# Meta keys of the attention turned by transposes, a Silu and a split moved ahead of the gates' casts, input squares on ScalarE

## The reference

```
h = rms_norm(x); z = h @ w_in
mix = [conv_mixer, pool_mixer, diff_attention(q, k, v)]
x = x + mix @ w_out
x = x + hier_moe(rms_norm(x))     # 16 experts, gates from a router
```

```
h = h + 0.5 * swiglu(rms_norm(h))
h = h + hybrid_mixer(rms_norm(h)) # three kinds of attention, 8 heads each, gates, two projections
h = h + 0.5 * swiglu(rms_norm(h))
```

## Time and profile before

| | |
|---|---|
| median of 3 runs | 1765.11 us (1764.02 to 1767.79) |
| profiled execution, its own time | 1767.74 us |
| its span | 1765.9 us |
| PE busy | 1740.2 us (99%) |
| DVE busy | 1197.1 us (68%) |
| ACT busy | 817.3 us (46%) |
| POOL busy | 237.9 us (13%) |
| mean granted clock of TensorE | 0.994 |
| moved by DMA | 288.80 MB, mean 164 GB/s |

### The profile page before, as it was taken

How to read it: one execution, slowest core, us unless ns; L and a number is a source line. 1 busy time by engine, 2 the same in 40 slices (tenths; PEclk the granted TensorE clock), 3 DMA queues, 4 the chain that set the end, 5 groups by cost and what they waited for, 6 DMA issues and landing times.

```text
span 1765.9 us, 37205 instructions
## 1 busy us (share of the span) xinstructions
PE 1740.2 (99%) x14096; PEld 1671.5 (95%) x14096; DVE 1197.1 (68%) x2082; ACT 817.3 (46%) x1308; POOL 237.9 (13%) x259
## 2 busy tenths in 40 slices
PE   8999999999999999999999999999999999999997
PEld 8998999999999998888999999999998888999997
DVE  7567756767665576666886655766567676887754
ACT  4555544444444333554554443444433445555443
POOL 1030000011000203212330002000111321340001
PEclk9999999999999999999999999999999999999999
DMA  7435555555555543342455555555554343555554
GB/s 266 130 108 177 189 180 184 186 180 184 173 177 169 178 156 129 111 132 96 162 180 171 177 171 175 175 170 168 182 175 136 105 158 105 167 176 183 188 180 132
DMA packets 84312, 288.80 MB, mean 164 GB/s; under 512 B 9072, under 2 KB 15984, under 8 KB 83952
## 3 DMA queue, kind: packets, MB, share of 16 engines
q1 hardware_dynamic: 79856, 283.14, 48.5%
q10 hardware_dynamic: 4352, 4.20, 0.8%
HBM read 285.96 MB, written 1.34 MB: 163 GB/s over the span
## 4 chain that ended last, share of the span: by engine, by line
PE 90%; DVE 5%; ACT 2%; issue 1%; DMA 0%; POOL 0%; SPq 0%; DVEq 0%; ACTq 0%
PE PS L857 27%; PE PS L859 27%; PE PS L858 27%; DVE w_lo L1512 2%; PE PS L1371 1%; PE PS L1334 1%; ACT w_hi L453 1%; PE PS L1374 1%; ACT S_all L733 1%; PE PS L1342 1%; PE PS L1360 1%; PE PS L1294 0%; PE PS L1352 0%; DMA raw<-stream 0%; PE PS L1051 0%
## 5 line engine op out<-in xcount | busy, mean ns | idle before, releaser
L1512 DVE TENSOR_TENSOR w_lo<-raw,w_hi 128x1024 fp32r<-128x1024 f32 x525 | 669.3, 1275 | 297.7 <-ACT w_hi L453 287.2
L857 PE MATMUL PS<-x_hi,w_hi 128*128 128x272 f32 (+1 forms) x2832 | 821.0, 290 | 3.1 <-DVE w_lo L1512 3.0
L859 PE MATMUL PS<-x_hi,w_lo 128*128 128x272 f32 (+1 forms) x2832 | 810.8, 286 | 0.0
L858 PE MATMUL PS<-x_lo,w_hi 128*128 128x272 f32 (+1 forms) x2832 | 808.8, 286 | 0.0
L453 ACT ACTIVATE w_hi<-raw 128x1024 fp32r<-128x1024 f32 x525 | 551.2, 1055 | 521.7 <-PE PS L859 514.4
L857 PEld LDWEIGHTS PS<-x_hi,w_hi 128*128 128x128 f32 x2832 | 535.8, 189 | 16.2 <-issue 14.0
L859 PEld LDWEIGHTS PS<-x_hi,w_lo 128*128 128x128 f32 x2832 | 536.4, 189 | 0.0
L858 PEld LDWEIGHTS PS<-x_lo,w_hi 128*128 128x128 f32 x2832 | 535.4, 189 | 0.7
L857 PE MATMUL PS<-a_hi,w_hi 128*128 128x272 f32 (+1 forms) x1280 | 364.8, 285 | 1.3 <-DVE a_lo L2142 1.3
L859 PE MATMUL PS<-a_hi,w_lo 128*128 128x272 f32 (+1 forms) x1280 | 363.7, 284 | 0.0
L858 PE MATMUL PS<-a_lo,w_hi 128*128 128x272 f32 (+1 forms) x1280 | 363.0, 284 | 0.0
(11 more groups left out here) (301 smaller groups left out, 1267.8 us busy)
## 6 DMA issues: line engine op xcount, KB each, us to landing
raw<-stream SPq DMA_DIRECT2D x525, 512.0 KB, 3.4
biasB<-rpbz ACTq DMA_DIRECT2D x16, 256.0 KB, 3.1
G<-b1mats SPq DMA_DIRECT2D x2, 1024.0 KB, 7.1
h<-xT SPq DMA_DIRECT2D x4, 272.0 KB, 5.7
out<-qk SPq DMA_DIRECT2D x4, 256.0 KB, 3.0
mat<-mats SPq DMA_DIRECT2D x1, 952.0 KB, 5.3
v_tok<-u_rows SPq DMA_DIRECT2D x4, 142.0 KB, 3.1
mat<-u_rows SPq DMA_DIRECT2D x4, 142.0 KB, 3.9
```

The costliest lines, as they stand in the source:

```text
L857: pe.matmul(ps, hi, rh, start=first, stop=False)
L858: pe.matmul(ps, hi, rl, start=False, stop=False)
L859: return pe.matmul(ps, lo, rh, start=False, stop=last)
L1512: dve.tensor_tensor(w_lo[:, slot, :], raw[:, slot, :], w_hi[:, slot, :].bitcast(F32), ALU.subtract).then_inc(lo_done, 1)
```

## The change

**Meta keys.** The second copy of the meta rows of the values goes: on PE the two matmuls of line 1303, on DVE the two copies of line 2011, and the clearing of `v_tok[64:128, 2]`. In `turn1` the four matmuls of line 1360 become four transposes that leave the 16 meta keys of both heads at partitions 0 to 15, 512 columns wide. DVE's copy `PT2` is 16 x 512 in place of 64 x 256. In `pv` two matmuls with 16 rows, one per head, take the place of the one with 64 rows.

**MoE's first turn.** On ACT the first Silu stands ahead of the cast of `gates_T`, and split 31 behind that cast, ahead of the four copies of gates. On DVE split 31 follows the low part of `gates_T`. DVE waits there for the first copy of gates only, and for the other three behind the first turn.

**Input squares.** ACT squares all eight tiles of the input between its casts of chunk 1 and chunk 2. POOL and DVE only add, three sums each.

```diff
@@ -194,6 +194,7 @@
         v_stage = qk[:, 8:10, 0:SEQ]
+        in_squares = qk[:, 8:16, :]
         UP, UQ, pooled_in = qk[:, 10:12, :], qk[:, 12:14, :], qk[:, 14:16, 0:SEQ]
@@ -203,8 +204,7 @@
         PT_b = [PT[:, 0:512], PT[:, 512:1024]]
-        PT2 = PT[:, 1024:1280]
-        MB = 64
+        PT2 = PT[:, 1024:1536]
         PTm, PTm2 = Gf[:, 22 * L:22 * L + 256], Gf[:, 22 * L + 256:22 * L + 384]
@@ -242,7 +242,7 @@
         cols_landed, consts_landed = sem("cols_landed"), sem("consts_landed")
-        warm_ready = sem("warm_ready")
+        warm_ready, x_squared = sem("warm_ready"), sem("x_squared")
         x_hi_done, x_lo_done = sem("x_hi_done"), sem("x_lo_done")
@@ -472,13 +472,13 @@
                     for s in range(4):
-                        if not (first and s < 2 and one_split):
+                        if not (first and s < 3 and one_split):
                             split_hi(c + (s + AHEAD), (slot0 + s + AHEAD) % RING)
...
                             finish(0, f, 1)
-                        if s % 2 == 1:
+                        if s % 2 == 1 and not (first and s == 1 and one_split):
@@ -510,9 +510,10 @@
                                scale=col[:, C_G + m:C_G + m + 1]).then_inc(x_hi_done, 1)
-            for n in range(1, AHEAD):
-                split_hi(n, n)
-
+            split_hi(1, 1)
+            for m in range(KD):
+                act.activation(in_squares[:, m, :], h[:, m, :], ACT.Square).then_inc(x_squared, 1)
+            split_hi(2, 2)
@@ -677,8 +678,11 @@
             split_hi(IN1 + OUT1 + 4, (IN1 + OUT1 + 4) % RING)
+            act.wait_ge(out_free, OUT1 + 1)
+            act.activation(S_sb[:, 0, 0, 0:SEQ], S_sb[:, 0, 0, 0:SEQ], ACT.Silu).then_inc(act_done, 1)
             act.wait_ge(aux_out, B1E["gates_turn", 0] + 1)
             act.activation(gates_T, PS[0:48, 5, 0:SEQ], ACT.Copy).then_inc(gates_hi, 1)
+            split_hi(IN1 + OUT1 + 5, (IN1 + OUT1 + 5) % RING)
@@ -1297,11 +1301,7 @@
                             pe.transpose(PS[:, b, P:2 * P], vs[:, P:2 * P], ident)
-                            pe.transpose(PS[0:META, b, 2 * P:3 * P], vs[:, 2 * P:L], ident)
-                            for u in range(2):
-                                r = MB + 32 * u
-                                mm = pe.matmul(PS[r:r + META, b, 3 * P:4 * P], vs[:, 2 * P:L], ident, start=True, stop=True,
-                                               skip_group_check=True)
+                            mm = pe.transpose(PS[0:META, b, 2 * P:3 * P], vs[:, 2 * P:L], ident)
                         elif what == "sumC":
@@ -1354,11 +1354,10 @@
                         pe.wait_ge(o_lo_done, l * PAIRS + p)
-                    for qt in range(2):
-                        for b in range(2):
-                            r = MB + 32 * b
-                            mm = pe.matmul(PS[r:r + META, 7, qt * P:(qt + 1) * P], S4[:, p % 2, b, qt, SEQ:L], ident,
-                                           start=True, stop=True, skip_group_check=True)
+                    for b in range(2):
+                        for qt in range(2):
+                            mm = pe.transpose(PS[0:META, 7, b * SEQ + qt * P:b * SEQ + (qt + 1) * P],
+                                              S4[:, p % 2, b, qt, SEQ:L], ident)
                     mm.then_inc(turned1_out, 1)
@@ -1369,10 +1368,12 @@
                             pe.matmul(PS[64 * b:64 * b + 64, 7, 0:SEQ], v_tok[:, kt, vc:vc + 64],
-                                      PT_b[b][:, kt * SEQ:(kt + 1) * SEQ], start=(kt == 0), stop=False, skip_group_check=True)
-                    vc = v_column(typ, t, 0)
-                    pe.matmul(PS[:, 7, 0:SEQ], v_tok[MB:P, 2, vc:vc + P], PT2[MB:P, :], start=False, stop=True,
-                              skip_group_check=True).then_inc(pv_out, 1)
+                                      PT_b[b][:, kt * SEQ:(kt + 1) * SEQ], start=(kt == 0), stop=False)
+                    for b in range(2):
+                        vc = v_column(typ, t, b)
+                        mm = pe.matmul(PS[64 * b:64 * b + 64, 7, 0:SEQ], v_tok[0:META, 2, vc:vc + 64],
+                                       PT2[0:META, b * SEQ:(b + 1) * SEQ], start=False, stop=True)
+                    mm.then_inc(pv_out, 1)
@@ -1598,6 +1599,8 @@
                 turn(cb, ob, 0, True)
+                if experts == 0:
+                    gates_cast(0)
                 with dve.Fori(1, tiles // 2) as i:
@@ -1632,15 +1635,13 @@
-            for m in range(KD // 2, KD):
-                to = half_acc if m == KD // 2 else half_sq
-                step(dve.tensor_tensor(to, h[:, m, :], h[:, m, :], ALU.mult))
-                if m > KD // 2:
-                    ins = dve.tensor_tensor(half_acc, half_acc, half_sq, ALU.add)
-                    if m < KD - 1:
-                        step(ins)
-                    else:
-                        ins.then_inc(half_summed, 1)
+            for m in range(KD // 2 + 1, KD):
+                dve.wait_ge(x_squared, m + 1)
+                ins = dve.tensor_tensor(half_acc, in_squares[:, m - 1, :] if m == KD // 2 + 1 else half_acc, in_squares[:, m, :], ALU.add)
+                if m < KD - 1:
+                    step(ins)
+                else:
+                    ins.then_inc(half_summed, 1)
             lam_in = col[0:64, C_LAM:C_LAM + 4].rearrange("p (a b) -> p a b", a=2)
@@ -1945,11 +1946,13 @@
                    .then_inc(aux_free, ax.up())
-                gates_cast(0)
+                split_lo(IN1 + OUT1 + 5, (IN1 + OUT1 + 5) % RING)
+                ax.up()
+                dve.wait_ge(aux_free, ax.now)
...
-                ax.up(4)
+                ax.up(4 if half else 3)
                 dve.wait_ge(aux_free, ax.now)
@@ -1961,8 +1964,6 @@
-            dve.memset(v_tok[MB:P, 2, :], 0.0).then_inc(setup_done, 1)
-            dve.wait_ge(setup_done, 2)
             dve.memset(biasB[:, :, :, SEQ:L], 0.0).then_inc(setup_done, 1)
@@ -2005,15 +2006,8 @@
                                                  PS[:, b, 0:2 * P].rearrange("p (k c) -> p k c", k=2)))
-                            step(dve.tensor_copy(v_tok[0:META, 2, i * P:(i + 1) * P], PS[0:META, b, 2 * P:3 * P]))
-                            for u in range(2):
-                                r, at = MB + 32 * u, 64 * u
-                                ins = dve.tensor_copy(v_tok[r:r + META, 2, i * P + at:i * P + at + 64],
-                                                      PS[r:r + META, b, 3 * P + at:3 * P + at + 64])
-                                if u == 0:
-                                    step(ins)
-                                else:
-                                    ins.then_inc(aux_free, ax.up())
+                            dve.tensor_copy(v_tok[0:META, 2, i * P:(i + 1) * P], PS[0:META, b, 2 * P:3 * P])\
+                               .then_inc(aux_free, ax.up())
                         elif what == "sumC":
@@ -2102,7 +2096,7 @@
                     dve.tensor_copy(PT_b[1], PS[:, 6, 0:512]).then_inc(probsT_dve, 1)
-                    dve.tensor_copy(PT2[MB:P, :], PS[MB:P, 7, 0:SEQ]).then_inc(probsT_dve, 1)
+                    dve.tensor_copy(PT2[0:META, :], PS[0:META, 7, 0:2 * SEQ]).then_inc(probsT_dve, 1)
@@ -2208,12 +2202,14 @@
             pool.wait_ge(setup_done, 1)
-            pool.wait_ge(lo_done, 2)
-            for i in range(2):
-                pool.wait_ge(h_landed[i], 16)
             pool.wait_ge(cols_landed, 16)
-
-            sum_squares(None, KD // 2)
+            for m in range(1, KD // 2):
+                pool.wait_ge(x_squared, m + 1)
+                ins = pool.tensor_tensor(acc, in_squares[:, 0, :] if m == 1 else acc, in_squares[:, m, :], ALU.add)
+                if m < KD // 2 - 1:
+                    step(ins)
+                else:
+                    ins.then_inc(squares_summed, 1)
```

## The result

The changed kernel took 1752.20 us (median of 4 runs, 1750.45 to 1752.92), the kernel before 1764.68 (4 runs, 1764.02 to 1767.79). The ratio is 0.9922, 95% interval 0.9909 to 0.9934: faster, by 0.66 to 0.91%. The forecast was 1752.5, in a range of 1747 to 1759. The profiled execution took 1752.92 around a span of 1751.1, and is the one to hold against the 1767.74 of before: 14.8 us less, where the sum said 14.3. Part of that agreement is chance, as the experiments show.

The account below looks back on a forecast made before the run. PE, busy 99% of the span, was taken as the bound. Value tiles 5.6, attention 1.0, MoE 4.0 and input 3.7 sum to 14.3 us off 1767.74, giving 1753.4; forecast 1752.5 for the median, range 1747 to 1759.

Parts of the forecast that it names:

- Value tiles: Twelve value tiles, six per layer: without the L1303 products each is 0.47 us shorter, 5.6 us in all, bounds 4.0 to 6.0.
- that rival: Value tiles: the saving isn't there because PE waits for splits instead, 1758 us; chance 0.03.
- Turning and products in a pair: Attention, 24 pairs: turning saves PE 0.40 us each; products with scores 0.12 worse in 13 pairs, 0.08 better in 11.
- 2.92 behind transposes only: Attention pair: the gate chunk behind the turning would take 2.92 us instead of 3.04, as behind transposes.
- The second copy: Attention: DVE's PT2 copy ends 0.25 us later and limits pv by each pair's slack; attention as a whole gains 1.0 us.
- The rival in which the wait doesn't bind: Attention: the wait for the copy doesn't bind, PE's whole side is saved, 1745 us; chance 0.08.
- MoE: MoE's first turn: table load and Silu fit before the gates' cast; PE's wait and half clock go, 4.0 us gained.
- Split 32: MoE: next in line on ACT, done 151.8 on ACT and 153.1 on DVE, needed 154.6; if late, 1.0 us lost.
- Input: Input stage: mean square 2.3 us earlier and full clock, 3.7 us gained, bounds 0 to 4; chunk 2 about 1.05 later.
- Half clock in new places: Whole execution: a listed sign that the prediction is wrong.
- two 1.4 us terms: Half clock taken to go behind the waits in MoE (1.45 us over 15 products) and input (1.4 us over 32 products).
- slower rival: Attention: PE's clock falls as eight transposes stand in a row, up to 1.7 us a fall, at most 1794; chance 0.03.

Follow-up runs that it names:

- run with two waits: Changed kernel, meta keys' transposes in other banks so the first four products of values wait only for DVE's first copy, the last two for its second: 1748.40 us, ratio 0.9904.
- second profile: The changed kernel run and profiled once more, nothing edited: median 1751.86 us, profiled execution 1749.86 us.
- later run: The changed kernel with ScalarE's split for chunk 2 moved ahead of its eight input squares: 1752.64 us, ratio 0.9921.
- copy doubled: The changed kernel with DVE's second copy of a pair (PT2, 16 x 512) made twice, one behind the other: 1770.12 us, ratio 1.0025.

## Why the prediction was right, point by point

**Value tiles: mechanism right, term too small.** 5.6 us in the sum, 6.26 measured (0.52 a tile). I had priced what remains at 0.3 us for three transposes; they took 0.25, as there is no switch in front of them: the second starts 0.11 behind the first, where in a pair, behind products, it is 0.16. No split held PE, so that rival fell.

**Turning and products in a pair: the step that failed is "2.92 behind transposes only".** The turning took 0.80 as said (1455.58 to 1456.38). But the chunk behind it lasts 3.01 to the products of values, not 2.92, because the first of these starts 0.09 late behind any chunk, waited for or not; my 2.92 was read ahead of transposes. Values and scores took 2.71 where I had 2.67. So PE's side saves 0.15 in a pair with scores at once, not 0.28. The run with two waits shows it bare: pairs of layer 1 at 9.86 us each, 10.01 before (1463.58 to 1473.59):

```profile
1475.78 1.08 PE L1374 MATMUL PS<-PT,v_tok 128*64 128x256 f32 x8
...
1485.63 1.08 PE L1374 MATMUL PS<-PT,v_tok 128*64 128x256 f32 x8
```

**The second copy: right that it binds, both sizes too large.** The sum had PE's side saving 8.9 us of attention (9.6 less 0.7) and the late copy taking 7.8 of it back, which left the 1.0. By the two-wait run PE's side saves 6.3 and the copy takes back 4.6; the changed kernel keeps 1.7. It came near because the two errors, 2.6 and 3.2 us, were against each other: what PE doesn't save, the copy can't take back. That is luck of the sum, not a term that was right. In layer 1 they cancel to nothing: 9.86 in some pairs, 10.13 and more in others. The rival in which the wait doesn't bind (1745) is what that run makes of it, 1748.4, since PE's saving is smaller.

**MoE: right at full clock (4.1 for 4.0), 2.6 in the profiled execution.** Table load and Silu fitted: the cast starts 0.44 us behind PE's transposes in both kernels (143.67 behind 143.23; before 146.58 behind 146.14). Split 32 was not late. What the prediction took for certain was that the half clock goes with the wait. It comes and goes between executions, and one of its places, 145.7, is just behind the idle of 1.18 us that the change leaves. "ScalarE: Activation LUTs" of the Trainium skill (What ACT_TABLE_LOAD costs) gives 2.66 us with a drain of 1.38. This case shows 1.3 from the load's start to Silu's, before (150.35 to 151.64) and after (142.01 to 143.31), and the cast no later; the measurement decides.

**Input: right at full clock (3.7 for 3.7), 2.4 in the profiled execution.** Squares 2.66 us at the low end of 2.6 to 3.4, chunk 2 about 1.0 later with 1.05 forecast, statistic at 19.88 for 19.8, mean square at 21.78 for 21.6. For the spread, 32.7 was forecast; it was 33.96 with chunk 5 at half clock, 32.47 in the second profile. The reason that the prediction gave for chunk 2's delay holds: squares, splits 2 and 3 and then the work that frees the bank stand in that order in ACT's queue, only that the bank is free with the square behind the copy. It was the later run's reading, the split alone, that failed.

**The clock.** "Half clock in new places" was named as a sign of being wrong. It was seen, and repeated profiles show that it isn't one: before has it in new places too. The right form of the two 1.4 us terms would have been a share of each, as half clock is back behind the new work in 6 of 9 profiles at either place, and before doesn't always pay for it. At full clock in these places the four terms measure 6.26 + 1.7 + 4.1 + 3.7 = 15.8; the profile set 1.5 from the stretch near 1372, which no term had, against 2.8 from the two that came. The medians, 1764.7 and 1752.2, lie 12.5 apart and average over this. That 1752.5 came within 0.3 us of the median is luck; the working supports the range, not the last microsecond.

**The slower rival** (the clock falls in attention) did not happen: neither profile of the changed kernel has a half clock there, with twice the transposes. "TensorE: Matmul & The Clock Gate" of the Trainium skill (Part 4, PE-mode transpose) says transposes don't count as PE-busy in the same way; eight of them, 0.80 us between chunks of 3 us, are no test of it, and no run here shows it.

## What to carry to other kernels

When a copy that a product waits for is made larger, price the wait with the cheapest test, the copy twice; if it binds, give the products that don't need it a wait of their own, which may need another bank for what it reads. A releaser in a profile is only the last of several: when the thing is moved and nothing changes, look for the other that ended within 0.1 us. And before a stretch of half clock is credited to a change, profile both kernels twice, for what a change seems to gain depends on which profile of before it is held against.

## What the runs showed of the hardware that I had not expected

VectorE's splits (SBUF to SBUF) and GpSimd's scalings of the probabilities keep each other out. In the kernel before, timelines of GpSimd and VectorE in one pair: the split lasts 1.91 us where others last 1.23, till 1.09 us behind the end of the second scaling (1473.91):

```profile
1471.77 2.14 POOL L2280 TENSOR_TENSOR S_all<-S_all,att 128x544 f32<-128x544 f32 x2 [7.87 <-DVE att L2088]
...
1473.09 1.91 DVE L1512 TENSOR_TENSOR w_lo<-raw,w_hi 128x1024 fp32r<-128x1024 f32 x1
```

In the changed kernel, in a pair of the same layer: now the split takes 1.20 and the two scalings 3.50:

```profile
1467.77 3.50 POOL L2276 TENSOR_TENSOR S_all<-S_all,att 128x544 f32<-128x544 f32 x2 [6.35 <-DVE att L2082]
...
1469.11 1.20 DVE L1513 TENSOR_TENSOR w_lo<-raw,w_hi 128x1024 fp32r<-128x1024 f32 x1
```

With the copy doubled the split starts (1476.01) only as the two scalings end (1473.95 and 2.14 us), and neither is longer: 1.20 and 2.14 us, while DVE's copies from PSUM beside them cost nothing.

Over all 48 scalings the mean is 1176 ns before, 1717 in the changed kernel and 1166 with the copy doubled. What the rows show to differ is when the split is reached, 0.27 us behind the second scaling's start before, 0.29 here, and clear of it with the copy doubled; which of the two gives way is not explained by that. None of the scalings is on the chain of waits above, and the page gives GpSimd 0% of the chain that ended last, before and after. "SBUF — State Buffer" of the Trainium skill (SBUF: two separate sides) has it that the one that starts first holds their shared port for the whole instruction. Before agrees; in the changed kernel the scaling's record begins 0.29 us ahead of the split's and yet the split isn't the one held up, so either the record's start is rough or the rule isn't the whole of it there.
